# Routing of both MoEs one token tile at a time, with the second MoE's last two accumulators opened behind its first gather

## The reference

```python
def hierarchical_moe(xn, w_router_group, b_router_group, w_router_expert, b_router_expert, w_gate, w_up, w_down):
    zg = (t @ w_router_group) + b_router_group
    pg_top, g_sel = lax.top_k(jax.nn.softmax(zg, axis=-1), 1)
    ze = jnp.einsum('td,gde->tge', t, w_router_expert) + b_router_expert
    ze_sel = jnp.take_along_axis(ze, g_sel[:, :, None], axis=1)[:, 0]
    v2, i2 = lax.top_k(ze_sel, TOP_K_INNER)
    gates = jax.nn.softmax(v2, axis=-1) * pg_top
    ...
    for e in range(N_EXPERTS_2):
        h = jax.nn.silu(t @ w_gate[e]) * (t @ w_up[e])
        y = y + combine[:, e:e + 1] * (h @ w_down[e])
```

## Time and profile before

| what | value |
|---|---|
| median of 3 runs | 948.72 us (948.4 to 950.57) |
| the profiled execution | 948.47 us, of which the span from first to last instruction is 946.7 us |
| PE busy | 798.7 us, 84% of the span |
| DMA, mean over the span | 328 GB/s |
| SP's queue (q1), the weights | 301.60 MB |
| DVE, ACT busy | 246.4 us, 163.5 us |

### The profile page before, as it was taken

One profiled execution on the slowest core, in us unless ns is written; L12 is line 12 of the kernel. 1 busy time (PEld: TensorE's weight loads), 2 busy tenths in 40 slices (PEclk: granted clock), 3 DMA queues, 4 the chain that ended last, 5 costly groups with the idle time before them and its releaser, 6 DMA issues.

```text
span 946.7 us, 20312 instructions
## 1 busy us (share of the span) xinstructions
PE 798.7 (84%) x9049; PEld 550.7 (58%) x9049; DVE 246.4 (26%) x640; ACT 163.5 (17%) x346; POOL 66.3 (7%) x73
## 2 busy tenths in 40 slices
PE   7999999999999989999998989558576576765765
PEld 4565688884676654446756777446454455544543
DVE  2142930231522221443535121102011020110201
ACT  2012222320411131205624000001000010000100
POOL 6200300000010030350000000000000000000000
PEclk9999999999999999999999999978899797888887
DMA  9985634059699999632657999999999999999996
GB/s 303 325 321 182 239 108 160 1 232 409 234 376 407 407 358 372 235 141 93 256 184 256 409 427 424 426 426 429 429 427 429 429 427 429 430 429 427 429 429 249
DMA packets 55556, 310.15 MB, mean 328 GB/s; under 512 B 5426, under 2 KB 7178, under 8 KB 43088
## 3 DMA queue, kind: packets, MB, share of 16 engines
q1 hardware_dynamic: 50848, 301.60, 79.8%
q0 software_dynamic: 2912, 4.37, 1.6%
q10 hardware_dynamic: 1744, 3.41, 0.9%
HBM read 307.76 MB, written 4.19 MB: 330 GB/s over the span
## 4 chain that ended last, share of the span: by engine, by line
PE 58%; DMA 38%; DVE 2%; issue 1%; ACT 0%; DVEq 0%; SPq 0%; ACTq 0%
PE ps L1630 54%; DMA ring<-in_w_up 27%; DMA ring<-in_w_down 5%; DMA ring<-in_w_gate 5%; PE ps L1656 1%; PE ps L1805 1%; PE ps L1945 0%; PE ps L1670 0%; DMA xx<-in_x 0%; PE ps L2057 0%; PE ps L1687 0%; PE ps L1767 0%; PE ps L1988 0%; DVE xx L1105 0%; PE ps L1678 0%
## 5 line engine op out<-in xcount | busy, mean ns | idle before, releaser
L1630 PE MATMUL ps<-ring,arena 128*32 128x128 f32 (+3 forms) x5792 | 276.6, 335 | 125.4 <-DMA ring<-in_w_up 46.4
L1630 PEld LDWEIGHTS ps<-ring,arena 128*32 128x32 f32 (+1 forms) x5792 | 195.6, 124 | 201.0 <-issue 71.4
L1630 PE MATMUL ps<-ring,xx 128*128 128x512 f32 (+2 forms) x384 | 156.1, 564 | 0.0
L1630 PE MATMUL ps<-arena 32*128 32x256 f32 (+11 forms) x1428 | 133.5, 369 | 5.4 <-issue 2.0
L1630 PEld LDWEIGHTS ps<-ring,xx 128*128 128x128 f32 x384 | 72.1, 190 | 74.9 <-issue 71.1
L1630 PEld LDWEIGHTS ps<-arena 128*32 128x32 f32 (+4 forms) x1428 | 85.8, 164 | 40.2 <-issue 33.4
L874 ACT ACTIVATE arena<-ps 128x128 f32<-128x128 f32 x40 | 11.1, 277 | 426.8 <-PE ps L1630 426.8
L1321 DVE TENSOR_TENSOR arena<-arena,ps 128x128 f32<-128x128 f32 x40 | 11.5, 288 | 277.8 <-ACT arena L874 277.8
L1630 PE MATMUL ps<-xx,ring 128*128 128x256 f32 x288 | 64.9, 382 | 0.0
L1630 PEld LDWEIGHTS ps<-xx,ring 128*128 128x128 f32 x288 | 53.9, 190 | 7.8 <-issue 0.7
L1630 PE MATMUL ps<-ring,xs 128*128 128x512 f32 x96 | 42.8, 604 | 0.0
(11 more groups left out here) (292 smaller groups left out, 575.7 us busy)
## 6 DMA issues: line engine op xcount, KB each, us to landing
ring<-in_w_up SPq DMA_DIRECT2D x38, 2048.0 KB, 25.2
ring<-in_w_gate SPq DMA_DIRECT2D x36, 2048.0 KB, 23.8
ring<-in_w_down SPq DMA_DIRECT2D x33, 2048.0 KB, 24.0
ring<-in_w_in SPq DMA_DIRECT2D x15, 2048.0 KB, 21.5
arena<-in_w_down SPq DMA_DIRECT2D x6, 2048.0 KB, 12.0
ring<-in_w_out SPq DMA_DIRECT2D x4, 2048.0 KB, 8.6
arena<-in_w_gate SPq DMA_DIRECT2D x3, 2048.0 KB, 12.2
arena<-in_w_up SPq DMA_DIRECT2D x2, 2048.0 KB, 15.3
```

The source lines that it names most:

```text
L1630: ins = pe.matmul(dst, w, x, start=start, stop=stop, skip_group_check=True)
```

## The change

The router's product, the norm factor and the search for the top group and experts are done tile by tile (`route_tile`, `norm_factors(m, tt)`), so that tile 0 is routed while PE still works on the last product. For the second MoE tile 0's transposes go into banks 0 and 2 (`tile_place`), which lets them run ahead of two products. The `ones` and `before` products are split by tile. A subtraction of 1 from `posm` is dropped (the row of numbers starts at 1 now, which costs an addition at the count of rounds), and another one moves behind `pick_slots`. In the second MoE accumulators 0 and 1 are opened before the positions and 2 and 3 behind the first gather. SP's load into `xx` waits for a new semaphore, `s_open`, in place of `s_pos`.

```diff
@@ sync @@
-            sp.wait_ge(s_pos, 2)
+            sp.wait_ge(s_open, 2)
             sp.wait_ge(s_xs, 6)
             load_moe2(8, 1, SECOND2[8], q1)
             for n in range(8, 12):
@@ scalar, norm_by_tile @@
+                        if k == 1:
+                            act.wait_ge(s_ms, ROOTS[f"x{m}", tt])
+                            act.activation(tile_stat(st_r, tt), tile_stat(st_a, tt), ACT.Sqrt).then_inc(s_rt, 1)
-                root(ROOTS[f"x{m}"])
-                act.wait_ge(s_rs, m)
                 for tt in range(TT):
+                    act.wait_ge(s_rs, FACTORS[f"x{m}", tt])
@@ vector @@
+            def route_tile(b, tt):
...
+                dve.wait_ge(s_rl, 2 * b + tt + 1)
+                step(dve.scalar_tensor_tensor(out=lg[b][:, tt, :], in0=bank(4, NR_COLS, tt * NR_COLS),
+                                              scalar=x_rstd[:, tt:tt + 1], in1=b_route[:, b, :], op0=ALU.mult,
+                                              op1=ALU.add))
+                step(dve.tensor_copy(gl[:, 0:NG], lg[b][:, tt, 0:NG]))
+                step(dve.max(m_tile, gl[:, 0:8]))
+                step(dve.tensor_copy(mg[:, 0:1], m_tile[:, 0:1]))
+                step(dve.match_replace(gr, mg, gl, PICKED))
+                step(dve.tensor_scalar(g_off, gr[:, 0:NG], PICKED, NEG, ALU.not_equal, ALU.mult))
+                step(dve.tensor_tensor(el[:, 0:NE].rearrange("p (g e) -> p g e", g=NG),
...
+                step(dve.max(m_tile, el[:, 0:NE]))
+                step(dve.tensor_copy(me[:, 0:2], m_tile[:, 0:2]))
+                step(dve.match_replace(er, me, el, PICKED))
+                dve.tensor_scalar(sel[b][:, tt, :], er[:, 0:NE], PICKED, None, ALU.is_equal).then_inc(s_sel, 1)
@@ vector, route @@
-                step(dve.tensor_scalar(posm[:, :, 0:NE], posm[:, :, 0:NE], -1.0, None, ALU.add))
-
+                pick_slots(b, 0)
                 step(dve.tensor_scalar(posm[:, :, NE:], posm[:, :, 0:2 * EG], -float(SLOTS), None, ALU.add))
                 dve.sem_inc(s_posm[b], 1)
-                pick_slots(b, 0)
...
                 step(dve.tensor_reduce(st_a[0:1, 4:5], bank(4, NE)[0:1], AX.X, ALU.max))
+                step(dve.tensor_scalar(st_a[0:1, 4:5], st_a[0:1, 4:5], float(SLOTS), None, ALU.add))
@@ tensor, out_product (first block) @@
+                        if (n, k) == (3, 2):
+                            router(0, 0)
...
-                router(0, 0)
+                open_accumulator(0, 0, 0)
                 norm_tile(1, 1)
@@ tensor, moe @@
                 router(b, 1)
...
-                    for part in range(4):
-                        mm(bank(part), ident, x_sb[:, :, part * T:(part + 1) * T], True, False)
-
-                pe.wait_ge(s_sel, b + 1)
+                    open_quarters((0, 1))
...
-                mm(bank(5, 2 * NE), before, sel[b][:, :, :], True, False)
-                mm(bank(5, NE, NE), ones, sel[b][:, 0, :], False, True).then_inc(s_pos, 1)
+                pe.wait_ge(s_sel, 2 * b + 1)
+                mm(bank(5, NE), before, sel[b][:, 0, :], True, True)
+                mm(bank(5, NE, NE), ones, sel[b][:, 0, :], True, False)
+                pe.wait_ge(s_sel, 2 * b + 2)
+                mm(bank(5, NE, NE), before, sel[b][:, 1, :], False, True).then_inc(s_pos, 1)
@@ tensor, group2 @@
                     gather(n)
-                    if not fresh:
+                    if fresh:
+                        open_quarters((2, 3))
+                    else:
                         scatter_expert(val(n * EG), EG - 1)
@@ tensor, second block @@
             branch_product(FOX, 1, 0, w_fox)
+            norm_tile(3, 0)
             branch_product(FOX, 1, 1, w_fox)
             read[0] += 1
             branch_product(DIL, 1, 0, w_dil)
-            pe.wait_ge(s_fo, 4)
-            norm_tile(3, 0)
+            router(1, 0)
             branch_product(DIL, 1, 1, w_dil)
-            router(1, 0)
+            read[0] += 1
             norm_tile(3, 1)
-            read[0] += 1
             moe(1, q1)
```

More of the change, by code:

```diff
@@ L337, in program @@
         s_cnt = sem("expert_counts")
+        s_open = sem("x_in_accumulators")
         s_pos = sem("route_positions")
@@ L653, in norm_bank, with tile_place, tile_written, tile_stat @@
             return 4
+        def tile_place(m, tt, k):
+            if (m, tt) == (3, 0):
+                return bank((0, 2)[k // 2 % 2], P, (2 * (k // 4) + k % 2) * P)
+            return bank(norm_bank(m) + k // 2, P, (k % 2) * T + tt * P)
+        def tile_written(m, tt, k):
+            return NTP0[m] + 4 * tt + (3 + k // 2 % 2 if (m, tt) == (3, 0) else k // 2 + 1)
+        def tile_stat(v, tt):
+            return v[:, 16 + tt:17 + tt]
         def x_ready(eng, m, tt):
@@ L1103, in norm_tile, with norm_factors @@
                 for k in (2, 3, 6, 7):
-                    dve.wait_ge(s_ntp, NTP0[m] + 4 * tt + k // 2 + 1)
-                    dve.tensor_scalar(xnT[:, k, tt * P:(tt + 1) * P],
-                                      bank(norm_bank(m) + k // 2, P, (k % 2) * T + tt * P),
-                                      gcol[:, row + k:row + k + 1], None, ALU.mult).then_inc(s_nev_d, 1)
-            def norm_factors(m):
-                dve.wait_ge(s_sq, 2 * m + 2)
-                rstd(f"x{m}", TT, D)
-                dve.tensor_copy(x_rstd, st_y[:, 0:TT]).then_inc(s_rs, 1)
-                dve.wait_ge(s_rs, m)
+                    if k == 6:
+                        a = tile_stat(st_a, tt)
+                        dve.wait_ge(s_sq, 2 * m + tt + 1)
+                        dve.tensor_scalar(a, a, 4.0 / D, 4 * EPS, ALU.mult, ALU.add).then_inc(s_ms, 1)
+                    dve.wait_ge(s_ntp, tile_written(m, tt, k))
+                    dve.tensor_scalar(xnT[:, k, tt * P:(tt + 1) * P], tile_place(m, tt, k),
+                                      gcol[:, row + k:row + k + 1], None, ALU.mult).then_inc(s_nev_d, 1)
+            def norm_factors(m, tt):
+                a, r, y, z = [tile_stat(v, tt) for v in (st_a, st_r, st_y, st_z)]
+                dve.wait_ge(s_rt, ROOTS[f"x{m}", tt])
+                dve.wait_ge(s_ms, ROOTS[f"x{m}", tt])
+                step(dve.reciprocal(y, r))
+                step(dve.tensor_tensor(z, a, y, ALU.mult))
+                step(dve.scalar_tensor_tensor(out=z, in0=z, scalar=-1.0, in1=y, op0=ALU.mult, op1=ALU.mult))
+                dve.scalar_tensor_tensor(out=x_rstd[:, tt:tt + 1], in0=z, scalar=3.0, in1=y, op0=ALU.add,
+                                         op1=ALU.mult).then_inc(s_rs, 1)
+                dve.wait_ge(s_rs, FACTORS[f"x{m}", tt])
             def group_norm(name, x, sq, g, n):
@@ L1248, in route @@
             def route(b):
-                gl, gr, el, er = route_g[b][:, :, 0, :], route_g[b][:, :, 1, :], route_e[b][:, :, 0, :], route_e[b][:, :, 1, :]
+                el = route_e[b][:, :, 0, :]
                 mg, me = route_m[b][:, :, 0, :], route_m[b][:, :, 1, :]
-                dve.wait_ge(s_rl, b + 1)
-                for tt in range(TT):
-                    step(dve.scalar_tensor_tensor(out=lg[b][:, tt, :], in0=bank(4, NR_COLS, tt * NR_COLS),
-                                                  scalar=x_rstd[:, tt:tt + 1], in1=b_route[:, b, :], op0=ALU.mult,
-                                                  op1=ALU.add))
@@ L1274, in route @@
-                note(dve.match_replace(er[:, 0, :], me[:, 0, :], el[:, 0, :], PICKED))
-                step(dve.match_replace(er[:, 1, :], me[:, 1, :], el[:, 1, :], PICKED))
-                dve.tensor_scalar(sel[b], er[:, :, 0:NE], PICKED, None, ALU.is_equal).then_inc(s_sel, 1)
                 step(dve.tensor_tensor(lg[b][:, :, 0:NG], lg[b][:, :, 0:NG], mg[:, :, 0:1].broadcast_to([P, TT, NG]),
@@ L1542, in _ @@
                     norm_tile(1, R_FFN, 0)
+                    norm_factors(1, 0)
+                    route_tile(0, 0)
             norm_tile(1, R_FFN, 1)
-            norm_factors(1)
+            norm_factors(1, 1)
+            route_tile(0, 1)
             route(0)
@@ L1612, in _ @@
             add_product(5, FOX, 1, 0, s_fo)
+            norm_tile(3, R_FFN2, 0)
+            norm_factors(3, 0)
             add_product(6, FOX, 1, 1, s_fo)
@@ L1615, in _ @@
             add_product(7, DIL, 1, 0, s_xn)
-            norm_tile(3, R_FFN2, 0)
+            route_tile(1, 0)
             add_product(8, DIL, 1, 1, s_xn)
             norm_tile(3, R_FFN2, 1)
-            norm_factors(3)
+            norm_factors(3, 1)
+            route_tile(1, 1)
             route(1)
@@ L1706, in router, with open_quarters, open_accumulator @@
                              k == 0, k == KD - 1)
-                if tt == 1:
-                    ins.then_inc(s_rl, 1)
+                ins.then_inc(s_rl, 1)
+            def open_quarters(parts):
+                for part in parts:
+                    ins = mm(bank(part), ident, x_sb[:, :, part * T:(part + 1) * T], True, False)
+                if part == 3:
+                    ins.then_inc(s_open, 1)
```

(5 more changed lines are left out.)

53 lines of the change are left out of this document (20 added, 33 removed).

## The result

The changed kernel takes 953.96 us (median of 7 runs, 952.1 to 956.79), the kernel before 949.63 in the same session (median of 7, 948.4 to 950.88). The ratio is 1.0048 [1.0038, 1.0058], slower by 3.6 to 5.5 us. The profiled execution took 953.61 us, its span is 951.8 us, 5.1 us more than before.

A forecast was written before the change was run, and what follows sets the result against it. The second MoE was taken as bound by a weight stream at 426 GB/s. First MoE +0.3 and second block +3.4 us gave +3.7 on the profiled 948.47, so 952.2, stated as a 952.3 us median; range 950.2 to 954.3.

The forecast's parts named there:

- The load into `xx`: Second MoE, SP: issued at 515.45 behind the last opening, it puts one 4.92 us weight into the full stream, 3.75 us later.
- the 515 to 516 and the less than 2 us: Signs of being right: load into `xx` issued at 515 to 516, ring load less than 2 us behind it.
- 0.35 came back: Weight stream, 518 to 530 us: a thin queue's loss partly saved by one more waiting weight, 0 to 0.9 us, 0.35 taken.
- Tile by tile: Before the second MoE: tile 0 routed early, tile 1's `sel` 0.4 us later, gather starting at 509.5 instead of 509.97.
- The logits at + 4.94: Second MoE: tile 1's router logits ready 4.94 us after the last product's end, at 505.7, and so the search start.
- a search of 2.5 us: Second MoE, DVE: searching tile 1 alone takes 2.5 us where both tiles took 3.54; 1.8 if time were per element.
- The gather's start at + 8.73: Second MoE, PE: gather starts at 509.5, with the last product's end forecast at 500.77.
- The first expert: Second MoE, PE: starts at about 515.1 behind gather and two openings, 0.6 us later than 514.44.
- The first MoE: First MoE: first expert at 254.8 instead of 254.49, +0.3 us, bounds -0.5 and +0.8.
- Within 0.3%: Rival, 0.20: same mechanism, but search nearer its width and the thin queue's whole loss back; +2.4 us, about 951.1.
- Faster: Rival, 0.05: stream has slack at 516, load into `xx` stays hidden, chain 3.2 us shorter over both MoEs; 945.5.
- Slower by more: Rival, 0.05: second MoE's first gather waits for ACT's late scaling of both tiles; +4.5 to +5.5 us, 953.7.

The follow-up runs named there:

- e2_load_late: Kernel before with one wait changed: SP's load into `xx` waits until the second MoE's first gather is done; 952.55 us, ratio 1.0036.
- e1_open_four: Changed kernel with all four second-MoE openings ahead of the positions again, the last releasing the load into `xx`; 951.11 us, ratio 1.0024.
- e6_load_last: Changed kernel with SP's load into `xx` moved behind the four first-group loads that followed it; 956.94 us, ratio 1.0072.
- e3_two_behind: Kernel before with only two second-MoE openings moved behind the first gather, the last releasing the load into `xx`; 954.8 us, ratio 1.0053.
- after: The changed kernel itself, against the kernel before; 953.96 us, ratio 1.0048.
- e4_again: The changed kernel, unaltered, run once more for a second profile; 954.09 us, ratio 1.0046 to the kernel before.
- e7_filled: Changed kernel with four useless products in PE's waits before the second MoE; 953.34 us, ratio 1.0039.
- e10_halves_kept: Changed kernel, second-MoE openings cut by tile, none behind the gather, one first-MoE opening moved earlier, start flag on tile 0's half alone; 949.01 us, ratio 0.9989.
- e5_halves: Changed kernel, second-MoE openings cut by tile, none behind the gather, one first-MoE opening moved earlier, start flag on both halves; 949.3 us, ratio 0.9991.

## Why the prediction was right, point by point

Direction and main cause were right: 952.3 us forecast, 953.96 measured, inside the range of 950.2 to 954.3; slower, because a load is issued later. The change cost 4.3 us in the medians of one session where 3.7 was forecast; of the 1.7 us between forecast and measurement 0.9 are the kernel before, which took 949.63 in that session and not 948.72. In the profile two falls of the clock of 1.6 us each, which the sum does not have, are in the measured time, and it lies 0.3 us under the range's upper end: that the range held is in part luck. (The sum itself gives 948.72 + 3.7 = 952.4, not 952.3; nothing hangs on that.) By its steps:

- **The load into `xx`** was the deciding term, and it is shown by adding it alone (`e2_load_late`), by putting the openings and so the load back (`e1_open_four`) and by pushing it further (`e6_load_last`). The load went out at 517.37 and the ring load 2.08 us behind it, outside the 515 to 516 and the less than 2 us that the prediction named as signs; the later first expert, below, is why. The forecast had the stream lose 3.75 us of which 0.6 were the first expert's and 0.35 came back: 2.8 us behind the first expert. Measured 2.28: 517.37 + 4.92 - 519.45 = 2.84 displaced, 0.56 given back (0.54 in `e2_load_late`). The 382 in place of 358 GB/s from 518 to 530 us fit that, but the window stands 2.8 us nearer to the start of the stream than before, so they don't measure it.
- **Tile by tile.** The last product was forecast to end at 500.77 plus 0.3 from the first MoE; it ended at about 501.5. The logits at + 4.94 and a search of 2.5 us: the search began at 506.34, so + 4.85, and took 2.50 (to 508.84). The gather's start at + 8.73: 510.15, so + 8.66. Cost per instruction and not per element was right.
- **The first expert** was forecast 0.6 us later (0.9 with the first MoE's share) and came 2.82 us later in the profile. This is the term that was mis-sized, and in it the gather, which the sum took over at 3.84 us: it took 5.47, 1.63 of it lost at the lower clock. I looked at what lies beside PE's waits, and not at whether the clock holds behind them. Some 0.4 us are the later end of the last product.
- **The first MoE** was forecast at +0.3 us. Taken from tile 0's transposes (231.84 before, 231.15 after) to the first expert (254.49, and 253.49 after) it got 0.3 us shorter, within the bounds given. Tile 0's transposes themselves started 0.7 us earlier, which is a difference between two executions, and the fall of the clock at 336 us (about 1.6 us) came on top. These three happen to leave the last product only 0.4 us later than forecast: that is luck. Which part of the front's loss is the program's and which the run's can't be settled from single profiles.
- **Rivals.** "Within 0.3%" needed the small terms to fall the other way; the search did not. "Faster" needed the load into `xx` before 511.7; it came at 517.37. "Slower by more" named the size almost (953.7), but not by its mechanism: ACT's scaling of both tiles started at 504.62, was done by 508.5, and the gather never waited for it.

## What to carry to other kernels

Where one engine issues all loads in a fixed order, a wait on a load is priced by the hole that it leaves in the stream, not by the engine that signals it: time issued, plus bytes over rate, against when the next load would be issued anyway. A transfer that hid in a gap costs more the later in the gap it starts: of 4.92 us here 1.6 with a lead of 2.79, 2.3 with 2.08, and all of it once it stands behind the gap (`e6_load_last`). When work is moved out of an engine's wait to shorten a path, ask both who waits for the moved work's end and what the bare wait does to that engine: here two openings that took 1.8 us on PE, moved out of a shadow where they cost nothing, cost 5.0 us on the kernel before (`e3_two_behind`), and putting them back won 2.3 of the change's 4.6 (`e1_open_four`). A fall of the clock counts in full only where the next work follows at once.

## What was not expected of the hardware

- **Short waits and the clock.** In the changed kernel, after waits of PE of 0.4 to 0.84 us each (2.4 us in all, spread over 8 us), the granted clock was 0.50 for about 3.5 us of uninterrupted products. A fall in the gather or just ahead of it is in all four profiles (after, `e3_two_behind`, `e4_again`, `e6_load_last`) of kernels that leave two openings behind the gather and do not fill the waits. It is not in `e7_filled`, the one profile that fills them. Of the other eight it is in one, `e10_halves_kept`, whose only waits there are of 0.50 and 0.40 us; `e5_halves` has the same waits to 0.01 us and did not fall, nor did `e1_open_four` after 0.84, 0.62 and 0.40. This suggests that waits have a part in it, and something that the trace doesn't show decides; one profile with the waits filled doesn't prove it.
- **The start flag works on the whole bank.** A product that starts an accumulation in columns 256 to 511 of a bank took away the accumulation that stood open in columns 0 to 255: what was added there next replaced the content (`e5_halves`), and with the flag on the first product alone both halves were kept (`e10_halves_kept`), at no cost in time. The Trainium skill (PSUM — Partial Sum Buffer, section on the four PSUM rules) states it: such a product clears the state of the whole 2 KiB bank on the partitions that it writes; these two kernels agree.
